# The head of a two-block transformer kernel: first weight chunks between the modulation chunks, three products in pieces, two modulation sums on TensorE

## What is computed

```python
c_act = jax.nn.silu(c)
mod = (c_act @ w_ada[l] + b_ada[l])[:, None, :]          # 1024 -> 6 x 1024
sh1, sc1, g1, sh2, sc2, g2 = jnp.split(mod, 6, axis=-1)
h = _rmsnorm(x, norm_g[l, 0]) * (1.0 + sc1) + sh1
y = _hybrid_mixer(h, w_in[l], ...)                       # begins with z = h @ w_in
...
x = x + g1 * _rmsnorm(y, norm_g[l, 1])                   # conv FFN, then GLA and
...                                                      # sliding-window attention
```

## Time and profile before

| | us |
|---|---|
| median of 3 runs | 820.62 |
| lowest, highest | 820.51, 820.77 |
| the profiled execution, its own time | 818.88 |
| its span, first to last instruction | 817.1 |
| TensorE busy in the span | 753.4 (92%) |
| VectorE busy | 540.1 (66%) |
| ScalarE busy | 400.3 (49%) |
| GpSimd busy | 107.2 (13%) |

### The profile page before, as it was taken

How to read it: one execution, slowest core, us unless ns; L and a number is a source line. 1 busy time by engine, 2 the same in 40 slices (tenths; PEclk the granted TensorE clock), 3 DMA queues, 4 the chain that set the end, 5 groups by cost and what they waited for, 6 DMA issues and landing times. The chain is left out here.

```text
span 817.1 us, 14365 instructions
## 1 busy us (share of the span) xinstructions
PE 753.4 (92%) x6052; PEld 735.6 (90%) x6052; DVE 540.1 (66%) x779; ACT 400.3 (49%) x540; POOL 107.2 (13%) x85
## 2 busy tenths in 40 slices
PE   2499998898789999999999999999999999999995
PEld 2499988898789899999999998999989999999994
DVE  4967978677564777777854555945676546566554
ACT  3275544455335455444453317717534565655533
POOL 0010000000040200000000060000004855343000
PEclk9699999999899999999999999979999999999998
DMA  9956365666434055555466534532444654324001
GB/s 353 417 225 202 108 245 228 248 232 257 143 139 159 1 202 194 193 188 188 158 262 238 189 107 155 178 133 59 148 155 148 209 199 139 120 103 156 2 1 52
DMA packets 20952, 139.57 MB, mean 171 GB/s; under 512 B 2356, under 2 KB 2996, under 8 KB 5016
## 3 DMA queue, kind: packets, MB, share of 16 engines
q1 hardware_dynamic: 20600, 137.80, 46.9%
q0 software_dynamic: 288, 0.85, 0.3%
HBM read 137.59 MB, written 1.05 MB: 170 GB/s over the span
## 5 line engine op out<-in xcount | busy, mean ns | idle before, releaser
L1452 PE MATMUL res<-hhi,whi 128*128 128x256 f32 (+1 forms) x1168 | 337.7, 289 | 6.2 <-DVE hlo L965 4.2
L929 DVE TENSOR_TENSOR wlo<-raw,whi 128x2048 fp32r<-128x2048 f32 (+1 forms) x106 | 238.6, 2252 | 141.4 <-ACT whi L579 139.3
L1453 PE MATMUL res<-hhi,wlo 128*128 128x256 f32 (+1 forms) x1168 | 331.6, 284 | 0.0
L1454 PE MATMUL res<-hlo,whi 128*128 128x256 f32 (+1 forms) x1168 | 331.4, 284 | 0.0
L579 ACT ACTIVATE whi<-raw 128x2048 fp32r<-128x2048 f32 (+1 forms) x106 | 197.8, 1868 | 160.8 <-issue 122.8
L1452 PEld LDWEIGHTS res<-hhi,whi 128*128 128x128 f32 (+1 forms) x1168 | 224.2, 192 | 8.8 <-issue 4.1
L1453 PEld LDWEIGHTS res<-hhi,wlo 128*128 128x128 f32 (+1 forms) x1168 | 224.1, 192 | 0.3
L1454 PEld LDWEIGHTS res<-hlo,whi 128*128 128x128 f32 (+1 forms) x1168 | 223.8, 192 | 0.2
L1452 PE MATMUL res<-uhi,whi 128*128 128x256 f32 x176 | 50.0, 284 | 1.0 <-ACT y L766 1.0
L1453 PE MATMUL res<-uhi,wlo 128*128 128x256 f32 x176 | 49.4, 281 | 0.0
L1454 PE MATMUL res<-ulo,whi 128*128 128x256 f32 x176 | 49.4, 281 | 0.0
(11 more groups left out here) (293 smaller groups left out, 1170.6 us busy)
## 6 DMA issues: line engine op xcount, KB each, us to landing
raw<-in_wts SPq DMA_DIRECT2D x100, 1024.0 KB, 5.0
raw<-in_w_ada SPq DMA_DIRECT2D x16, 1024.0 KB, 4.8
gates<-in_w_ada SPq DMA_DIRECT2D x6, 1024.0 KB, 8.2
raw<-in_wts SPq DMA_DIRECT2D x4, 768.0 KB, 7.3
y<-in_w_ada SPq DMA_DIRECT2D x2, 1024.0 KB, 10.7
x<-in_xT SPq DMA_DIRECT2D x2, 512.0 KB, 6.3
outT<-x SPq DMA_DIRECT2D x4, 256.0 KB, 2.4
biasA<-in_relb SPq DMA_DIRECT2D x1, 768.0 KB
```

The source lines that it names most:

```text
L929: nc.vector.tensor_tensor(wlo[c % SPL][:, 0:b], raw[RAW_OF["w", c] % RAW][:, 0:b], whi[c % SPL][:, 0:b].bitcast(f32), ALU.subtract).then_i ...
L1452: mm(out, ah, bh, start=first, stop=False)
L1453: mm(out, al, bh, start=False, stop=False)
L1454: return mm(out, ah, bl, start=False, stop=last)
```

## The change

It touches the first 60 us; the rest of the program is the same, instruction for instruction. (Two semaphores, `gth_ready` and `sth_ready`, on which nobody waited, give way to the new ones.)

- Transfers: `cols` and ada chunk 0 go ahead of `x`; the order of ada chunks is 0, 4, 5, 1, 6, 2, 7, 3; weight chunk QC stands after ada 1 and QI after ada 2; `ident` and `rope1` follow ada 3, then KK and MISC, and the other mixer constants stand ahead of the fifth weight chunk (QA).
- Ada chunks 5 and 6 are laid out with the contraction on the partitions and are summed by TensorE, `mod_product`: 16 products each of a 128 x 128 block with one column of silu(c), `ccs`, which ScalarE makes. VectorE adds the bias from PSUM. Six chunks are left to VectorE.
- The scaled input is made in other places: GpSimd multiplies `x` with `rstd` in four instructions into `sq`; ScalarE applies `pcol` and the shift in one instruction for a tile into `tb`, and makes `hhi` from that; VectorE's eight instructions of L1050 are gone.
- `warm(20)` is gone. The products of QC, QI and KK are cut: QC on tiles 0 to 3, QC on 4 and 5, QI on 0 to 5, QC on 6 and 7, QI on 6 and 7, KK on all.
- ScalarE: `high(0)` after the tiles 0 and 1, `high(1)` after 4 and 5, `high(2)` after 6 and 7. VectorE: `low(0)`, `low(1)`, `low(2)` follow suit.

```diff
-ADA_FIRST = (0, 4, 1, 5, 2, 6, 3, 7)
+ADA_FIRST = (0, 4, 5, 1, 6, 2, 7, 3)
+ADA_PE = (5, 6)
-STREAM = [("ada", a) for a in ADA_FIRST[:6]] + [("w", 0)] + [("ada", a) for a in ADA_FIRST[6:]]
+STREAM = [("ada", 0), ("ada", 4), ("ada", 5), ("ada", 1), ("w", 0), ("ada", 6), ("ada", 2), ("w", 1), ("ada", 7), ("ada", 3)]
...
# GpSimd
+            pool.wait_ge(rstd_known["n1"], 1)
+            for j in range(4):
+                nc.gpsimd.tensor_tensor(sq[:, 2 * j:2 * j + 2, :], x[:, 2 * j:2 * j + 2, :],
+                                        rstd[:, None, :].to_broadcast([P, 2, T]), ALU.mult).then_inc(xr_ready, 1)
...
# ScalarE
-            split_hi("n1", tb, lambda k: mod[:, k:k + 1], range(6))
-            high(0)
-            split_hi("n1", tb, lambda k: mod[:, k:k + 1], range(6, KT))
-            for c in range(1, SPL):
-                high(c)
+            for j in range(4):
+                act.wait_ge(xr_ready, j + 1)
+                act.wait_ge(ada_used, ada_done((0, 1, 2, 3)[j]))
+                act.wait_ge(pcol_ready, j + 1)
+                for k in (2 * j, 2 * j + 1):
+                    nc.scalar.activation(tb[:, k, :], sq[:, k, :], ACT.Identity, bias=mod[:, k:k + 1],
+                                         scale=pcol[:, 0, k:k + 1]).then_inc(scaled["n1"], 1)
+                split_hi("n1", tb, None, (2 * j, 2 * j + 1))
+                if j != 1:
+                    high((0, 0, 1, 2)[j])
...
# VectorE: scale_columns(j) waits for mod_product or ada(4 + j), adds the bias
# of a chunk of TensorE's, and makes pcol
+            ada(0)
+            ada(4)
+            scale_columns(0)
+            norm_rstd("n1")
+            ada(1)
+            scale_columns(1)
+            split_lo("n1", tb, None, (0, 1))
+            low(0)
+            split_lo("n1", tb, None, (2, 3))
+            ada(2)
+            scale_columns(2)
+            split_lo("n1", tb, None, (4, 5))
+            low(1)
+            ada(7)
+            scale_columns(3)
+            ada(3)
+            split_lo("n1", tb, None, (6, 7))
+            low(2)
...
# TensorE
-            pe.wait_ge(ident_in, 16)
-            pe.wait_ge(ada_used, ada_done(6))
-            warm(20)
+            def mod_product(a):
+                wait_ada(pe, a)
+                pe.wait_ge(c_ready, 2)
+                n = ADA_PE.index(a)
+                w = ada_buffer(a).rearrange("p (k n) -> p k n", k=KT)
+                for i in range(2):
+                    for k in range(KT):
+                        last = mm(pT[:, 512 * n + i:512 * n + i + 1], w[:, k, i * P:i * P + P], ccs[:, k:k + 1],
+                                  start=k == 0, stop=k == KT - 1)
+                last.then_inc(mod_done, 1)
+            for a in ADA_PE:
+                mod_product(a)
+            for c, ks in ((QC, range(4)), (QC, (4, 5)), (QI, range(6)), (QC, (6, 7)), (QI, (6, 7)), (KK, range(KT))):
+                early(c, ks)
```

More of the change, by code:

```diff
@@ L66 @@
 NADA = 24
-ADA_FIRST = (0, 4, 1, 5, 2, 6, 3, 7)
+ADA_FIRST = (0, 4, 5, 1, 6, 2, 7, 3)
+ADA_PE = (5, 6)
 ADA_FIRST_AT = (0, 1, 2, "y", 0, 1, 2, "y")
 ADA_AFTER = {ZG + i: 8 + i for i in range(12)} | {DOWN + 3 * i: 20 + i for i in range(4)}
-ADA_ORDER = list(ADA_FIRST) + [ADA_AFTER[c] for c in sorted(ADA_AFTER)]
+ADA_ORDER = [a for a in ADA_FIRST if a not in ADA_PE] + [ADA_AFTER[c] for c in sorted(ADA_AFTER)]
 def kt_of(c):
@@ L232, in build @@
         cact = sb("cact", [P, D])
+        ccs = sb("ccs", [P, KT])
         pcol = sb("pcol", [P, 4, 8])
@@ L432, in _ @@
             sp.dma_start(cact[:, :], crow_d).then_inc(c_in, 16)
-            for k in range(0, KT, 4):
-                sp.dma_start(x[:, k:k + 4, :], xT[:, k:k + 4, :]).then_inc(x_in, 16)
             sp.dma_start(cols[:, :], cols_d).then_inc(const_in, 16)
@@ L1036, in _, with scale_columns @@
             dve.wait_ge(c_ready, 1)
-            for j in range(4):
-                ada(j)
-                if j == 3:
-                    low(0)
-                ada(4 + j)
-                if j == 0:
-                    norm_rstd("n1")
-                else:
-                    split_lo("n1", tb, lambda i: mod[:, i:i + 1], range(2 * j - 2, 2 * j))
-                dve.wait_ge(ada_used, ada_done(4 + j))
-                own(nc.vector.scalar_tensor_tensor(pcol[:, 0, 2 * j:2 * j + 2], mod[:, 8 + 2 * j:10 + 2 * j], 1.0,
-                                                   col("norm_g", 2 * j, 2), ALU.add, ALU.mult))
-                for k in (2 * j, 2 * j + 1):
-                    nc.vector.scalar_tensor_tensor(tb[:, k, :], x[:, k, :], pcol[:, 0, k:k + 1], rstd[:, :],
-                                                   ALU.mult, ALU.mult).then_inc(scaled["n1"], 1)
-            split_lo("n1", tb, lambda i: mod[:, i:i + 1], (6, 7))
-            for c in range(1, SPL):
-                low(c)
+            def scale_columns(j):
+                a = 4 + j
+                if a in ADA_PE:
+                    i = ADA_PE.index(a)
+                    dve.wait_ge(mod_done, i + 1)
+                    own(nc.vector.tensor_tensor(mod[:, 2 * a:2 * a + 2], pT[:, 512 * i:512 * i + 2], col("b_ada", 2 * a, 2), ALU.add))
+                else:
+                    dve.wait_ge(ada_used, ada_done(a))
+                nc.vector.scalar_tensor_tensor(pcol[:, 0, 2 * j:2 * j + 2], mod[:, 2 * a:2 * a + 2], 1.0,
+                                               col("norm_g", 2 * j, 2), ALU.add, ALU.mult).then_inc(pcol_ready, 1)
+            ada(0)
[16 more added lines that the diff above has]
+            low(2)
             own(nc.vector.memset(fones, 1.0))
@@ L1083, in _ @@
                 if b == MISC:
+                    dve.wait_ge(mixc_in, 64)
                     for h in range(4):
@@ L1667, in _, with early @@
             mean("n1", sq, range(KT), squares["n1"], KT)
-            pe.wait_ge(ident_in, 16)
-            pe.wait_ge(ada_used, ada_done(6))
-            warm(20)
-            for c in range(NC):
+            def mod_product(a):
[8 more added lines that the diff above has]
+                last.then_inc(mod_done, 1)
+            def early(c, ks):
+                wait_weights(c)
+                for k in ks:
+                    pe.wait_ge(in_lo["n1"], k + 1)
+                    for i in range(2):
+                        last = half_product(c, i, k, res[c], hhi, hlo, None, i == 0 and k == 0, i == 1 and k == KT - 1)
+                if k == KT - 1:
+                    last.then_inc(product_done, 1)
+            for a in ADA_PE:
+                mod_product(a)
+            for c, ks in ((QC, range(4)), (QC, (4, 5)), (QI, range(6)), (QC, (6, 7)), (QI, (6, 7)), (KK, range(KT))):
+                early(c, ks)
+            for c in range(KK + 1, NC):
                 if c < BRANCH:
-                    if c == QC:
-                        fm(c, hhi, hlo, None, lambda k: pe.wait_ge(in_lo["n1"], k + 1), range(KT))
-                    elif c == MISC:
+                    if c == MISC:
                         wh, wl = weights(c)
@@ L1905 @@
     relb = np.ascontiguousarray(np.concatenate([table[:, r] for r in rel], axis=2).transpose(1, 0, 2))
+    w_ada = a["w_ada"][0].reshape(D, 24, 2, P).transpose(1, 3, 2, 0).reshape(24, P, 2 * D).copy()
+    for n in ADA_PE:
+        w_ada[n] = a["w_ada"][0][:, 256 * n:256 * n + 256].reshape(KT, P, 256).transpose(1, 0, 2).reshape(P, 2 * D)
     W = (a["w_in"][0], a["w_branch"][0], a["w_out"][0], a["w_up"][0], a["w_down"][0], a["gla_w_in_2"][0],
```

46 lines of the change are left out of this document (30 added, 16 removed).

## The result

| | before | changed |
|---|---|---|
| first comparison, median (lowest to highest) | 820.69 us (820.51 to 821.26, 4 runs) | 816.21 us (815.68 to 817.52, 4 runs) |
| ratio, 95% interval | | 0.9942 (0.9925 to 0.9959) |
| second comparison | 820.42 us (817.69 to 823.18, 30 runs) | 818.93 us (816.31 to 821.21, 10 runs) |
| ratio, 95% interval | | 0.998 (0.9962 to 0.9998) |
| profiled execution: time, span | 818.88, 817.1 us | 815.68, 813.9 us |

The first comparison, which the prediction was about, came out 4.5 us faster, under the range of 816.8 to 822.0. The second, of the same two kernels, came out 1.5 us faster. In it the kernel before spreads over 5.5 us and the changed one over 4.9. Of the 3.0 us between the two answers 2.7 lie in the changed kernel's medians, 816.21 and 818.93. That spread turned out to be the larger half of the story.

What follows compares the result with a forecast made beforehand. VectorE was taken to bound the start by putting off TensorE's products. The new chain ends KK 4.2 us earlier, the shared port takes back 3.05, leaving 1.15: 820.62 - 1.15 = 819.4 us, range 816.8 to 822.0.

Steps and rivals of the forecast that it cites:

- What bounds the start: First 60 us: VectorE delays TensorE; the port shared with GpSimd leaves 3.05 us of delay, KK's end gains 1.15 us.
- Rival A: Start: the shared port does not meet VectorE's sums; gain 3.1 us (817.5), or 4.2 (816.4) without any collision; chance 0.27.
- `rstd` at 19.4: Start: with `x` landed at 11.4, squares, mean, guess and Newton step end at 19.4 us.
- TensorE's sums in 4.2 us: Start: each of TensorE's two modulation sums takes 4.2 us, and both end before VectorE asks.
- rival B: Start: the granted clock stays at 1.2 GHz until KK, which ends 2 us later than before: 822.6; chance 0.12.
- Rival B's decisive point: Before KK: a low clock decides only once the QC and QI pieces end after `low(2)`, at 50.4 us.
- `warm(20)` costs nothing: Start of the kernel before: the 20 warming products lay in a wait of TensorE and cost nothing.
- I take a shift of KK's end as a shift of the whole: After KK: nothing later hangs on absolute time, so KK's gain of 1.15 us reaches the program's end.
- a difference of over 0.5 us in this span: KK's end to program's end: expected 759.8 us as before; more than 0.5 us off means the shift step was wrong.
- the transfers have slack by then: After the start: transfers hold nothing up, so a shift of KK's end passes on whole.
- The centre, 819.4: Whole kernel: likeliest median, 820.62 less 1.15 us, given as 818.8 to 820.1; chance 0.48.
- The range of 5.2 us: Whole kernel: 816.8 to 822.0 us, leaving out the far end of rival A and most of rival B.

Runs made afterwards that it cites:

- a_again: The changed kernel run once more, unchanged, with a second profile: 818.93 us, 0.998 against the kernel before.
- a_small: The changed kernel with each of the 16 later ada transfers cut from 128 x 2048 to 128 x 128 elements: 813.16 us, 0.9918 against the kernel before.
- a_wfirst: The changed kernel with 12 swaps in the transfer order, each weight chunk asked for ahead of its modulation chunk: 811.03 us, 0.9888 against the kernel before.
- the two shifted pairs: Both kernels with four or eight warming products put between KK and MISC: before 821.09 and 820.42 us, changed 822.71 and 823.99 us.
- the small pair: The kernel before and the changed one, both with the 16 later ada transfers cut to 128 x 128 elements: 812.98 and 813.16 us.
- the wfirst pair: The kernel before and the changed one, both with 12 weight chunks asked for ahead of their modulation chunks: 812.06 and 811.03 us.
- b_nowarm: The kernel before without its 20 warming products: 820.34 us, 1.0008 against 819.80 us.

## Why the prediction failed, step by step

**What bounds the start: right, and mis-sized.** `low(0)` was to start near 27.5 to 28 and did at 27.77; the sums of ada 1 were to take over 2 us against 1.28 and took 2.40 and 2.27. KK's end was put at 56.15 with a gain of 1.15 us; it was 56.44 and 0.87. The Trainium skill ("SBUF — State Buffer", section "Who interferes with whom") says that such a pair of instructions excludes each other; by that rule the sums had to be hit, and the trace agrees with 2.40 against 1.28 us. Rival A is out. The first comparison's number alone would have said the opposite: 816.21 is next to the 816.4 that rival A gives for no collision at all. That nearness is luck.

**`rstd` at 19.4: too early, and no longer covered.** In the changed kernel it was ready at 20.3. `x` had landed for the squares at 11.88 instead of 11.4, and from there to the guess's start it took 6.59 us instead of 6.15. Its Newton step starts with ScalarE's guess, at 18.97 in the first profile, and 18.48, 19.84 and 19.45 in a_again, a_small and a_wfirst. In the kernel before, that chain had slack behind two sums of VectorE. Now it is on the path, and its jitter of over a microsecond goes into the start. The jitter is TensorE's: the mean of the squares, the same 16 records, takes 5.99 us in the first profile, 5.19 in a_again and 6.61 in a_small:

```profile
12.44 5.99 PE L1573 MATMUL pX<-sq,meanw 128*128 128x256 f32 x16 [12.44 <-ACT sq L639]
12.75 5.19 PE L1573 MATMUL pX<-sq,meanw 128*128 128x256 f32 x16 [12.75 <-ACT sq L639]
12.68 6.61 PE L1573 MATMUL pX<-sq,meanw 128*128 128x256 f32 x16 [12.68 <-ACT sq L639]
```

Its first records take 0.63 us each and its last 0.38; that looks like the clock coming up at different moments, but these traces hold no granted clock for the first part of it. At `wlo` 12 the changed kernel was ahead of its partner by 0.90, 0.62, 0.66, 1.13, -0.04 and 0.34 us (first profile, a_again, the two shifted pairs, the small pair, the wfirst pair).

**TensorE's sums in 4.2 us: wrong, for lack of the clock.** At the upper level a sum takes 3.63 us (the first one of a_again), near the 3.4 us of the estimate by loads alone. The second took 6.99 us at the lower one, as rival B had feared for the pieces. In the first profile it ends at 31.2, ahead of VectorE's need at 33.05, so it cost nothing. My sum came out right because of cover, not because of the price. Rival B's decisive point (pieces later than `low(2)`) wasn't reached.

**`warm(20)` costs nothing: right**, by b_nowarm.

**"I take a shift of KK's end as a shift of the whole": this is the step that failed.** From KK's end to the span's end the kernel before has 759.8 us, the changed one 757.5 (813.9 - 56.44), and 763.0 in its second profile (819.4 - 56.39). The prediction had named a difference of over 0.5 us in this span as the sign that the step was wrong. The runs show in its place a stage, 103 to 206 us, whose length isn't fixed: 103.18 us before, 101.19 and 106.44 in two profiles of the changed kernel, with TensorE idle for 10.8 to 11.3 us in all three and its clock at 0.97, 1.00 and 0.94. Of the 3.2 us between the profiled executions, KK's end gives 0.87 and the stage 2.0. That "the transfers have slack by then" is what was wrong: from 103 us on ScalarE waits for them, and TensorE's clock may or may not fall behind such a wait.

I had looked at the transfers up to 60 us and found slack, and let that stand for the whole program. A look at the waits for DMA between 105 and 205 us, which the profile of before had, would have told of 9.1 us that hang on when transfers land, and of a clock that fell twice there. The centre, 819.4, is near the 818.93 of the larger comparison, but a sum that had nothing in it for such a stage can take no credit for that. The range of 5.2 us round it was too narrow on the fast side for four executions with mostly short stages. I had taken the spread from three runs, 0.26 us, although the profiled execution of the same kernel stood 1.74 us under them, and I used that distance as a constant; thirty later runs spread over 5.5 us.

**What the change is worth by itself.** With the stage out of the way it is 1.03 us in the wfirst pair (812.06 against 811.03) and -0.18 in the small pair (812.98 against 813.16), four runs each. The starts say -0.04 to 1.13. At a recorded clock of 0.976 the second comparison has three executions of each, 817.72 to 818.33 us before and 816.31 to 817.53 changed. So it is worth about 1 us, on few runs. Whether the changed kernel also makes long stages rarer isn't settled: the two stages profiled of it were 101.19 and 106.44 us.

## What to carry to other kernels

A queue that issues in order passes on the latest of its waits. Where two streams share it, look in its rows for a transfer that goes out long after its own buffer was free, and put the stream whose buffers come free sooner ahead. Before a shift of the start is taken as a shift of the end, list every later wait whose releaser is a DMA: each is a place where the shift can vanish or grow. And an idle engine that takes work over isn't free when it reads what the busy one reads; here handing the scaling back to VectorE was worth more than the help.
